# Scan time steps on four column groups with a summing product, and changes of order, banks and queues around it

## The chip, the core and the metric

The kernel runs on one core of one Trainium2 chip. The metric is the device time of one execution in microseconds. Everything is float32. The engines are TensorE (PE, with its weight loads PEld), VectorE (DVE), ScalarE (ACT), GpSimd (POOL) and SyncE (SP), which only issues transfers. Results of TensorE go to eight PSUM banks of 512 columns.

## The reference, cut to what matters

One layer of a decoder step, for a prompt of 256 tokens and eight sampled sequences of 4 tokens (288 columns together):

```
hn   = rmsnorm(h);  proj = hn @ w_in            # z 1024, xbc 1536, dt 16, q/k/v 512 each
xbc  = silu(causal_conv(xbc, conv_state))
dt   = softplus(dt_raw + dt_bias);  a = -exp(a_log)
y    = chunked scan (SSD) of x, dt, a, B, C from state s0; new state is an output
y    = rmsnorm((y + x * d_skip) * silu(z))
att  = block-sparse attention over own keys and paged past keys (1024 per sequence)
h   += concat(y, att) @ w_out
h   += cross attention of rmsnorm(h) over 256 memory tokens, 4 heads, @ w_ca_o
h   += square(relu(rmsnorm(h) @ w_up)) @ w_down
y_prompt, y_sample = rmsnorm(h)
```

Outputs beside y: keys and values of prompt, sample and memory, the convolution histories and the scan states. dt_raw, the "time steps" of the title, is a product of hn (1024 x 288) with 1024 x 16 weights: one value per head and token.

## The kernel before

The activations lie transposed, 128 channels on the partitions and 288 token columns. A dense "tile" is one 128-channel output: eight matmuls of 128 rows x 128 columns of weights against 288 columns of hw (four or eight in the output projections), accumulated in one bank, evicted by VectorE. Weights come in blocks of 1 MB into a ring of four slots (wring), issued by SyncE. In the trace one float32 matmul is two records.

Everything is hand-scheduled: `make_plan` writes one sequence (SEQ) of tiles and items, and each engine walks the same sequence and issues its part of each item. So moving an item moves it on all engines. Small TensorE results go through "turns" (`turn`, `plan_turns`): each turn takes the least recently used bank of a set and waits until that bank's turn before has been evicted by ScalarE or VectorE; the set is TURN_BANKS (2, 3, 6) at the start, FEW_BANKS during the key scores. Banks 0 and 1 alternate for the tiles.

The stages in order, with the names of the items:

- Opening: WARM matmuls of ones into bank 7; ident, x and norm_mix are loaded (L877 to L885); TensorE transposes x (L1146), ScalarE squares it, GpSimd sums the squares (L1001), VectorE scales it by norm_mix into hw (L2080).
- q tiles (L1189), `memt` (transposes of the memory tokens; VectorE scales them, L2080, then ScalarE squares them, L1827, both reading the bank), `ss x` (sum of squares over partitions, L1490, then square root on ScalarE and reciprocal on VectorE, L2152), `qrep` (replication of q, L1577). The q tiles are evicted by two pairs of instructions (L2092, L2094).
- Key scores of the paged keys (L1208, transposed by VectorE, L2229) between tiles of k, memory and x; x tiles are followed by the convolution on VectorE.
- `V` units (L1255): attention probabilities times paged values, four sequences side by side on four column groups of 32.
- `dt`: eight matmuls with wdt (128 x 16 stationary, 288 moving, L1496), then a series on VectorE for softplus, beside the z tiles.
- The scan: `tok` (transposes to token rows), `sums`, `seg`, `yo`, `upd`; `kvtok` writes keys and values as token rows (L1152, L2076) into staging buffers, from which GpSimd stores them (L984). `stage` has two buffers, sq and ohT, so the third group of tokens (sample) uses sq again and waits until the first store out of it has landed (kst_out 0).
- `zsq`: ScalarE squares the gated z and multiplies by the norm's gain (L1827, L1992); `ss ssd`, `inv ssd` (L2152) give the norm's factor. `head self n` is prompt attention; `pvown`/`pvout` combine (L2201) and turn the sampled attention; `state` adds the new scan state (L2380, L2381), `sf` transposes it for the store; `oz`, `oa` tiles are the output projection.
- Cross attention, then the MLP in a form with seven half-width products of sums instead of eight (L1603). Its operands need sums of hw (activation_sum, L2454) and of weights (L2443 and following). VectorE makes the sums of hw while the last output tiles (`cao`) come in.

## Time and profile before

| | us |
|---|---|
| timed runs, median of 3 (lowest to highest) | 657.47 (657.03 to 658.47) |
| the profiled execution: time | 659.61 |
| its span | 658.0 |
| TensorE busy | 631.4 |
| VectorE busy | 404.8 |
| ScalarE busy | 153.5 |
| GpSimd busy | 139.6 |

The span is what the trace covers. Busy times overlap across engines. The mean granted clock of TensorE was 0.991 of full speed. The page's slices show TensorE at nine tenths or more from the second slice to the last but one.

### The profile page before, as it was taken

How to read it: one execution, taken by the hardware profiler on the slowest of the kernel's cores; microseconds unless marked ns; L12 is line 12 of the kernel's file. 1: busy time of each engine (PE TensorE's matmuls, PEld its weight loads, DVE VectorE, ACT ScalarE, POOL GpSimd, SP SyncE). 2: the span in 40 equal slices, each digit the busy share in tenths (PEclk: the TensorE clock that was granted, in tenths of full speed). 3: DMA queues.
4: the chain of work that ended last, by engine and by line, in shares of the span. 5: the costliest groups of instructions: out<-in, count | busy, mean ns of one | idle time of the engine just before them, and what ended most of it. 6: DMA issues, size and time to landing. Idle time of an engine off the chain costs nothing.

```text
span 658.0 us, 13121 instructions
## 1 busy us (share of the span) xinstructions
PE 631.4 (96%) x4879; PEld 505.2 (77%) x4879; DVE 404.8 (62%) x880; ACT 153.5 (23%) x409; POOL 139.6 (21%) x221
## 2 busy tenths in 40 slices
PE   8899999999999999889999999999999999999995
PEld 6656776676676565446757876799999999999995
DVE  2565576997654766685523255878788883644733
ACT  4110020010213974582112433121121110000001
POOL 6142112210310026051001200425344350000000
PEclk8999999999999999899999999999999999999998
DMA  8898878898841259875786653245454454544501
GB/s 297 249 308 266 299 249 271 274 292 244 233 121 65 65 192 293 275 177 152 238 281 256 216 176 120 74 133 179 128 175 147 148 174 161 181 140 133 176 13 73
DMA packets 98636, 125.75 MB, mean 191 GB/s; under 512 B 6428, under 2 KB 74544, under 8 KB 98579
## 3 DMA queue, kind: packets, MB, share of 16 engines
q1 hardware_dynamic: 92930, 106.81, 50.1%
q0 software_dynamic: 5648, 18.14, 8.8%
q8 instruction: 39, 0.64, 0.4%
q14 instruction: 19, 0.15, 0.1%
HBM read 116.63 MB, written 8.31 MB: 190 GB/s over the span
## 4 chain that ended last, share of the span: by engine, by line
PE 73%; DVE 5%; POOL 2%; DMA 2%; issue 1%; ACT 1%; DVEq 0%; POOLq 0%; ACTq 0%
PE ps L1603 33%; PE ps L1189 24%; PE ps L1146 3%; PE ps L1255 3%; DMA out_prompt_k<-sq 2%; PE ps L1208 1%; PE ps L1421 1%; PE ps L1367 1%; POOL acc L1001 1%; PE ps L1303 1%; PE ps L1297 1%; PE ps L1496 1%; PE ps L1411 1%; PE ps L1372 1%; PE ps L1230 1%
## 5 line engine op out<-in xcount | busy, mean ns | idle before, releaser
L1189 PE MATMUL ps<-hw,wring 128*128 128x288 f32 x576 | 148.3, 414 | 0.7 <-DMA wring<-in_w_in 0.6
L1189 PEld LDWEIGHTS ps<-hw,wring 128*128 128x128 f32 x576 | 108.3, 192 | 37.2 <-issue 6.9
L2229 DVE STREAM_TRANSPOSE tmp<-big 128x1024 f32<-128x1024 f32 x32 | 37.9, 1222 | 2.5 <-PE ps L1208 1.9
L1603 PE MATMUL ps<-hw,wring 128*128 128x144 f32 x256 | 34.2, 287 | 1.6 <-DVE hw L2080 1.6
L1001 POOL TENSOR_TENSOR acc<-acc,sq 128x288 f32<-128x288 f32 (+1 forms) x35 | 29.5, 844 | 24.9 <-ACT sq L1827 22.5
L1603 PEld LDWEIGHTS ps<-hw,wring 128*128 128x128 f32 x256 | 32.5, 190 | 2.0 <-DVE hw L2080 2.0
L1603 PE MATMUL ps<-big,wring 128*128 128x144 f32 x256 | 34.0, 286 | 0.0
L2076 DVE COPY tmp<-ps 128x512 f32<-128x512 f32 (+6 forms) x34 | 20.8, 617 | 19.9 <-PE ps L1146 16.1
L1189 PE MATMUL ps<-big,wring 128*128 128x288 f32 x128 | 32.7, 409 | 0.0
L1189 PE MATMUL ps<-attT,wring 128*128 128x288 f32 x128 | 31.9, 407 | 0.7 <-DVE hT L2125 0.7
L1603 PEld LDWEIGHTS ps<-big,wring 128*128 128x128 f32 x256 | 32.4, 190 | 0.0
L1820 ACT ACTIVATE tmp<-ps 128x512 f32<-128x512 f32 (+5 forms) x37 | 20.2, 560 | 49.2 <-PE ps L1146 37.7
L2019 ACT ACTIVATE big<-big 128x288 f32<-128x288 f32 x32 | 13.0, 444 | 74.5 <-DVE big L2641 74.5
L1189 PEld LDWEIGHTS ps<-big,wring 128*128 128x128 f32 x128 | 23.9, 190 | 7.8 <-issue 1.8
L1189 PEld LDWEIGHTS ps<-attT,wring 128*128 128x128 f32 x128 | 24.0, 190 | 7.1 <-DVE hT L2125 0.9
L1189 PE MATMUL ps<-tmp,wring 128*128 128x256 f32 x128 | 29.5, 385 | 0.0
L2622 DVE TENSOR_TENSOR tmp<-ps,xc 128x144 f32<-128x144 f32 x64 | 18.2, 305 | 17.5 <-PE ps L1603 16.4
L832 POOL DMA_DIRECT2D big<-in_cache_k x28 | 15.3, 545 | 63.5 <-issue 63.5
L1124 POOL TENSOR_TENSOR tmp<-big 128x144 f32<-128x144 f32 x16 | 15.5, 969 | 61.9 <-ACT big L2019 61.9
L1189 PEld LDWEIGHTS ps<-tmp,wring 128*128 128x128 f32 x128 | 23.8, 190 | 5.8 <-issue 2.5
L1603 PE MATMUL ps<-tmp 128*128 128x144 f32 x192 | 24.8, 286 | 0.0
L1603 PE MATMUL ps<-tmp,xc 128*128 128x144 f32 x192 | 24.8, 286 | 0.0
(347 smaller groups left out, 1154.3 us busy)
## 6 DMA issues: line engine op xcount, KB each, us to landing
wring<-in_w_in SPq DMA_DIRECT2D x16, 1024.0 KB, 6.8
wring<-in_w_up SPq DMA_DIRECT2D x16, 1024.0 KB, 5.1
wring<-in_w_down SPq DMA_DIRECT2D x16, 1024.0 KB, 4.7
big<-in_cache_v SPq DMA_DIRECT2D x56, 256.0 KB, 3.6
big<-in_cache_k SPq DMA_DIRECT2D x36, 256.0 KB, 3.8
big<-in_cache_k POOLq DMA_DIRECT2D x28, 256.0 KB, 4.5
wring<-in_w_out SPq DMA_DIRECT2D x6, 1024.0 KB, 6.2
wring<-in_w_ca_kv SPq DMA_DIRECT2D x4, 1024.0 KB, 8.7
```

The lines of the kernel that those rows point to most:

```text
L832: e.dma_start(big[:, ds(i * 512 + (n % 2) * 4096, 512)], cache[ds(page, 1)].rearrange("o p n -> p (o n)")).then_inc(signal[n % 2], 16)
L1001: pool.tensor_tensor(a, a, sq[:, m % 2, 0:n], ALU.add).then_inc(acc_done, 1)
L1124: step(pool.tensor_tensor(ff_sums[:, 0, n], a[1], a[0], ALU.subtract))
L1146: last = pe.transpose(ps[0:c, bank(key), col:col + r], in_, ident[0:r, 0:r])
L1189: last = pe.matmul(ps[:, BANK[key], 0:width], w, rhs, start=(k == 0), stop=(k == K_TILES[kind] - 1))
L1255: last = pe.matmul(ps[32 * b:32 * b + 32, PV_BANKS[s], :], p[:, 32 * b:32 * b + 32], src[:, b, t, :], start=((first or again) and t == 0), ...
L1603: last = pe.matmul(ps[:, bank_, col * HALF:(col + 1) * HALF], w(k), x(k), start=(start and k == 0), stop=(stop and k == 3))
L1820: last = act.activation(dst, src, ACT.Copy)
L2019: act.activation(ff[:, c * T:(c + 1) * T], ff[:, c * T:(c + 1) * T], ACT.Square).then_inc(ff_done, 1)
L2076: last = dve.tensor_copy(dst, src)
L2229: dve.transpose(KT_[:, step_ % 2].rearrange("p c (w j) -> p w c j", j=32), src[:, :, :, m, :])\
L2622: return dve.tensor_tensor(w[:, row, half * HALF:half * HALF + HALF], product, part_, ALU.add)
```

## The change

- `dt` is split. A new item `dt_part` stands between the two halves of x tile 5: matmul k goes to column group k mod 4 (32 columns each), so bank rows 0 to 31 hold the part sum of k = 0 and 4, rows 32 to 63 that of 1 and 5, and so on. VectorE copies the bank to vv. At the old place one matmul with a constant 0/1 matrix (dt_sum, 128 x 16) adds the four groups. wdt moves from its own buffer into ohT, padded to 32 columns with zeros that GpSimd sets.
- WARM goes from 12 to 10. ident, x_sample and norm_mix are loaded through ScalarE's queue, and ScalarE computes one square root of a constant at the start, so that its table is loaded there.
- The opening's turns use four banks (2, 3, 6, 7); `memt 0` stands ahead of `ss x`.
- `stage` gets a third buffer, osb; VectorE's wait for kst_out 0 goes, and a wait for kst_out 2 moves from `zsq` on ScalarE to `pvown 0` on VectorE.
- `zsq 0` ahead of `seg 1 3`; `inv ssd` behind `pvout 0`; `oz 0 1` ahead of `sf`.
- The sums 2 and 3 of hw are made once for all four blocks after the last tile, instead of for three blocks ahead of it and one behind.

```diff
-WARM = 12
+WARM = 10
     item("probs", 0)
     pair("x", 4)
     unit("V", 0, 0)
-    pair("x", 5)
+    tile("x", 5, 0)
+    item("dt_part")
+    tile("x", 5, 1)
...
-BANKS_NOW = [TURN_BANKS]
+BANKS_NOW = [[2, 3, 6, 7]]
...
-            IN_SCORES.append(LAST_IN_BANK[6])
+            IN_SCORES.extend(LAST_IN_BANK[b] for b in (6, 7))
...
-        stage = [sq[:, :, :].rearrange("p s t -> p (s t)")[:, 0:512], ohT[:, :]]
+        stage = [sq[:, :, :].rearrange("p s t -> p (s t)")[:, 0:512], ohT[:, :], osb]
...
-            elif kind == "ktok" and key[1] == 2:
-                e.wait_ge(kst_out[0], 16)
...
+                elif s[0] == "dt_part":
+
+                    pe.wait_ge(dtw_in, 16)
+                    pe.wait_ge(wdt_clear, 1)
+                    bank_free(pe, "dt_part")
+                    for k in range(DT):
+                        r = slice(32 * (k % 4), 32 * (k % 4) + 32)
+                        last = pe.matmul(ps[r, bank("dt_part"), 0:T], wdt[:, k, :], hw[:, k, :], start=(k < 4),
+                                         stop=(k >= 4), tile_position=(0, 32 * (k % 4)))
+                    last.then_inc(turn_ps, 1)
                 elif s[0] == "dt":
-                    pe.wait_ge(dtw_in, 16)
+                    turned(pe, "dt_part")
+                    pe.wait_ge(const_in, 16 * 11)
                     tile_bank_free(pe, "dt")
-                    for k in range(DT):
-                        last = pe.matmul(ps[0:SH, BANK["dt"], 0:T], wdt[:, k, :], hw[:, k, :], start=(k == 0), stop=(k == DT - 1))
-                    last.then_inc(dense_ps, 1)
+                    pe.matmul(ps[0:SH, BANK["dt"], 0:T], dt_sum[:, :], vv[:, :], start=True, stop=True).then_inc(dense_ps, 1)
...
+            act.dma_start(ident[:, :], I["ident"]).then_inc(ident_in, 16)
+            for i in range(2):
+                cols = slice(512 * i, 512 * i + 512)
+                act.dma_start(xin[0:NS, 2, cols], I["x_sample"][:, cols]).then_inc(x_in[i], 16)
+                if i == 0:
+                    act.dma_start(vec_rows[0:DT, :], I["norm_mix"].rearrange("(r n) -> r n", n=P)).then_inc(mix_in, 16)
+
+            act.wait_ge(zeros_made, 2)
+            act.activation(small[:, 95:96], eps_t[:, :], ACT.Sqrt)
...
-                    activation_sum(2, 0, 3)
-                    activation_sum(3, 0, 3)
                     step(activation_sum(0, 3, 4))
                 elif c == 7:
                     dve.wait_ge(hw_done, 16 + 8)
                     activation_sum(1, 3, 4).then_inc(hs_made, 1)
                     dve.wait_ge(hs_made, 1)
-                    activation_sum(2, 3, 4)
-                    activation_sum(3, 3, 4).then_inc(hs_made, 1)
+                    activation_sum(2, 0, 4)
+                    activation_sum(3, 0, 4).then_inc(hs_made, 1)
```

TensorE around the time steps, before (L1189 are tiles, eight matmuls each; L1255 is a V unit; L1496 the time steps):

```order
L1189 MATMUL ps<-hw,wring 128x288 x16
L1255 MATMUL ps<-big,qs 32x512 x8
L1189 MATMUL ps<-hw,wring 128x288 x16
L1255 MATMUL ps<-big,qs 32x512 x8
L1496 MATMUL ps<-hw,wdt 16x288 x8
L1189 MATMUL ps<-hw,wring 128x288 x40
```

and now (L1194 are the tiles, L1261 the V units, L1505 the part sums, L1512 the summing product):

```order
L1194 MATMUL ps<-hw,wring 128x288 x16
L1261 MATMUL ps<-big,qs 32x512 x8
L1194 MATMUL ps<-hw,wring 128x288 x8
L1505 MATMUL ps<-hw,ohT 32x288 x8
L1194 MATMUL ps<-hw,wring 128x288 x8
L1261 MATMUL ps<-big,qs 32x512 x8
L1512 MATMUL ps<-vv,tmp 16x288
L1194 MATMUL ps<-hw,wring 128x288 x40
```

The eight part products have moved up between two x tiles, and one product is left behind the V unit.

VectorE after the first prompt heads, before (L2407 to L2409 the bounds of a head, L2152 the reciprocal of the scan's norm, L2201 the combination of sampled attention that TensorE transposes next):

```order
L2407 TENSOR_REDUCE mx<-tmp 128x1
L2408 TENSOR_REDUCE mx<-tmp 128x1
L2409 TENSOR_SCALAR mx<-mx 128x2
L2152 RECIPROCAL rstd<-rstd 128x288
L2201 TENSOR_TENSOR tmp<-ps,qs 128x512
L2076 COPY attT<-ps 64x256
```

and now (L2225 is that combination, L2175 the reciprocal, L2147 the first use of its result):

```order
L2433 TENSOR_SCALAR mx<-mx 128x2
L2225 TENSOR_TENSOR tmp<-ps,qs 128x512
L2099 COPY attT<-ps 64x256
L2438 RECIPROCAL mx<-mx 128x2
L2444 TENSOR_SCALAR tmp<-tmp,mx 128x128
L2444 TENSOR_SCALAR tmp<-tmp,mx 128x256
L2428 SCALAR_TENSOR_TENSOR tmp<-ps,tmp 128x384
L2431 TENSOR_REDUCE mx<-tmp 128x1
L2432 TENSOR_REDUCE mx<-tmp 128x1
L2433 TENSOR_SCALAR mx<-mx 128x2
L2175 RECIPROCAL rstd<-rstd 128x288
L2147 TENSOR_TENSOR vv<-ps,rstd 128x288
```

The reciprocal has moved behind the combination and the next head's bounds, to just ahead of its use.

TensorE at the transposes of the new state, before (L1146 x8 are the transposes, the L1189 row after them is tile oz 0 1):

```order
L1279 MATMUL ps<-kT,qz 128x256
L1146 MATMUL ps<-ident,tmp 128x128 x8
L1189 MATMUL ps<-big,wring 128x288 x8
L1255 MATMUL ps<-big,qs 32x512 x8
L1303 MATMUL ps<-tmp,vtok 64x128 x3
```

and now (L1151 the transposes, L1194 the tile):

```order
L1285 MATMUL ps<-kT,qz 128x256
L1194 MATMUL ps<-big,wring 128x288 x8
L1151 MATMUL ps<-ident,tmp 128x128 x8
L1261 MATMUL ps<-big,qs 32x512 x8
L1309 MATMUL ps<-tmp,vtok 64x128 x3
```

The tile has moved ahead of the transposes.

## Rows read from the trace of the kernel before

**Rows 1.** The page: busy time, share and instructions of each engine.

```profile
PE 631.4 (96%) x4879; PEld 505.2 (77%) x4879; DVE 404.8 (62%) x880; ACT 153.5 (23%) x409; POOL 139.6 (21%) x221
```

**Rows 2.** Waits of TensorE: who waited, for whom, total us, times, longest.

```profile
PE ps L1146 <- ACT sq L1827: 3.3, 2, 1.6
PE ps L1152 <- DVE sq L2076: 2.6, 1, 2.6
PE ps L1146 <- DVE tmp L2381: 1.6, 1, 1.6
PE ps L1603 <- DVE hw L2080: 1.6, 1, 1.6
...
PE ps L1146 <- DVE tmp L2201: 0.9, 1, 0.9
...
PE ps L1490 <- POOL acc L1001: 0.7, 1, 0.7
...
PE ps L1189 <- DMA wring<-in_w_in: 0.6, 1, 0.6
```

**Rows 3.** Timeline of the opening: start, us, engine, line, operation, idle before.

```profile
1.17 4.43 PE L1440 MATMUL ps<-ones 128*128 128x128 f32 x24 [1.17 <-POOL eps_t L1004]
...
3.72 0.43 SPq L854 DMA_DIRECT2D wring<-in_w_in  x1
...
6.96 0.46 DVE L2076 COPY hT<-ps 128x288 f32<-128x288 f32 x1 [0.99 <-PE ps L1146]
...
10.94 5.84 PE L1189 MATMUL ps<-hw,wring 128*128 128x288 f32 x16 [0.55 <-DMA wring<-in_w_in]
```

**Rows 4.** Stretches: busy of each engine, then granted clock, DMA share, GB/s.

```profile
10.00:15.00 5.00, 4.45 (x13) 3.06 (x12) 1.62 (x5) 3.25 (x6) 4.28 (x6) 0.66 1.06 394
255.00:282.00 27.00, 23.52 (x142) 12.22 (x141) 17.20 (x36) 13.49 (x34) 3.14 (x7) 0.94 0.83 262
```

**Rows 5.** Timeline of 25 to 60, at the replication of q.

```profile
31.78 0.86 DVE L2092 TENSOR_TENSOR qz<-ps,rstd 64x256 f32<-64x256 f32 x2 [2.36 <-PE ps L1189]
...
34.51 1.93 PE L1577 MATMUL ps<-qs,ident 128*32 128x256 f32 x32
```

**Rows 6.** Timeline of 160 to 210, at the time steps.

```profile
164.47 1.92 PE L1255 MATMUL ps<-big,qs 128*32 128x512 f32 x16
...
166.22 4.04 PE L1496 MATMUL ps<-hw,wdt 128*16 128x288 f32 x16
...
170.19 20.06 PE L1189 MATMUL ps<-hw,wring 128*128 128x288 f32 x80
...
182.22 7.57 PEld L1189 LDWEIGHTS ps<-hw,wring 128*128 128x128 f32 x32 [0.58 <-DVE big L2103]
```

**Rows 7.** Timeline of 236 to 285, behind the copy of the sample keys.

```profile
265.46 0.68 DVE L2076 COPY sq<-ps 32x512 f32<-32x512 f32 x1 [4.04 <-DMA out_prompt_k<-sq]
...
268.27 2.07 PE L1367 MATMUL ps<-tmp,later 128*128 128x512 f32 x2
...
269.58 1.23 DVE L2288 TENSOR_TENSOR tmp<-tmp,ex 128x1024 f32<-128x1024 f32 x1 [1.17 <-ACT ex L1881]
```

**Rows 8.** Timelines of 274 to 284 and 282 to 352: ScalarE's idle time, the reciprocal.

```profile
280.09 0.60 ACT L1899 ACTIVATE tmp<-ps 128x512 f32<-128x512 f32 x1 [3.39 <-PE ps L1367]
...
292.65 1.94 DVE L2152 RECIPROCAL rstd<-rstd 128x288 f32<-128x288 f32 x1
```

**Rows 9.** Timeline of 404 to 436, VectorE ahead of the first MLP chunk.

```profile
425.90 1.20 DVE L2454 TENSOR_TENSOR kT<-hw,vtok 128x432 f32<-128x432 f32 x1
...
427.84 0.37 DVE L2080 TENSOR_SCALAR hw<-hT,vec 128x288 f32<-128x288 f32 x1
```

**Rows 10.** Value pages: SyncE's issues, TensorE's use, and the page's median landing.

```profile
312.36 23.00 SPq L841 DMA_DIRECT2D big<-in_cache_v  x16
...
339.00 1.93 PE L1255 MATMUL ps<-big,qs 128*32 128x512 f32 x16
...
big<-in_cache_v SPq DMA_DIRECT2D x56, 256.0 KB, 3.6
```

More of the change, by code:

```diff
@@ L148, in make_plan @@
     tile("qk", 0, 1)
+    item("memt", 0)
     item("ss", "x")
-    item("memt", 0)
     tile("qk", 1, 0)
@@ L237, in make_plan @@
     unit("V", 0, 2)
+    item("zsq", 0)
     item("seg", 1, 3)
-    item("zsq", 0)
     item("yo", 1, 2)
@@ L249, in make_plan @@
     item("head", "self", 0)
-    item("inv", "ssd")
     item("pvown", 0)
@@ L253, in make_plan @@
     item("pvout", 0)
+    item("inv", "ssd")
     tile("oz", 0, 0)
@@ L257, in make_plan @@
     item("head", "self", 2)
+    tile("oz", 0, 1)
     item("sf")
-    tile("oz", 0, 1)
     unit("V", 1, 0)
@@ L424, in plan_turns @@
             turn("conv")
+        elif s[0] == "dt_part":
+            turn("dt_part", "dve")
         elif s[0] == "kvtok":
@@ L582, in build @@
         cvin = part(1536)[0:NB * 3, :]
+        dt_sum = part(SH)
         CS = tmp[:, 0:1024].rearrange("p (s t) -> p s t", s=2)
@@ L605, in build @@
         ebuf = ohT[:, :]
+        wdt = ohT[:, 0:DT * 32].rearrange("p (k n) -> p k n", k=DT)
         at[0] = xpad_at
@@ L740, in bank_free @@
                 turned(e, BEFORE_IN_BANK[key])
-            elif bank(key) in UP_BANKS:
+            elif bank(key) in UP_BANKS[:2]:
                 e.wait_ge(up_done, 16)
@@ L914, in load_constants @@
                     sp.dma_start(hcol[:, i:i + 1], I[name].rearrange("(h o) -> h o", o=1)).then_inc(const_in, 16)
-                sp.dma_start(wdt[:, :, :], w_in[:, IN_DT:IN_DT + SH].rearrange("(k p) n -> p k n", p=P))\
+                sp.dma_start(wdt[:, :, 0:SH], w_in[:, IN_DT:IN_DT + SH].rearrange("(k p) n -> p k n", p=P))\
                     .then_inc(dtw_in, 16)
@@ L1007, in _ @@
             pool.memset(qw, 0.0).then_inc(qw_clear, 1)
+            pool.memset(wdt[:, :, SH:32], 0.0).then_inc(wdt_clear, 1)
             add_squares("x", T)
@@ L1070, in _ @@
                         turned(pool, (outs[0][0], g))
-                        store(kd, stage[g % 2][0:n, :] if s[0] == "kvtok" else mstage[0:n, g],
+                        store(kd, stage[g][0:n, :] if s[0] == "kvtok" else mstage[0:n, g],
                               kst_out[g if s[0] == "kvtok" else 3 + g])
@@ L1196, in key_steps @@
                     if k == 0 and g == 0:
-                        turned(pe, IN_SCORES[0])
+                        for key in IN_SCORES:
+                            turned(pe, key)
                         tile_done(pe, ("qk", 0, 1))
@@ L1698, in turn_targets @@
                 return xKT[:, u[1], c, 2 * w:2 * w + 2, :], ps[:, b, :].rearrange("p (b t) -> p b t", b=2)
+            if kind == "dt_part":
+                return vv[:, :], ps[:, b, 0:T]
             if kind == "qrep":
@@ L2200, in take_result @@
                     if s == 0:
+                        dve.wait_ge(kst_out[2], 16)
                         dve.tensor_tensor(osb, ps[:, 7, :], qsf[:, 0:512], ALU.add).then_inc(pv_out, 1)
@@ L2556, in _ @@
                     self_bounds(s[1])
+                elif s[0] == "dt_part":
+                    leave("dt_part")
                 elif s[0] == "dt":
```

17 lines of the change are left out of this document (7 added, 10 removed).

## The prediction

> **What bounds the kernel now.** I read the page first: TensorE is busy for 631.4 of 658.0 us [rows 1]. So time can only come from shorter matmul work, from TensorE's few waits, or from its clock. The waits of TensorE come next [rows 2]: seven lines, 11.3 us. The reader is to see that each is named by one producer, and that four producers (the squares of ScalarE, the copy to sq, the new state, the down-scaled hw) are other engines' instructions that stand behind something TensorE doesn't need yet. Then the timeline around each of them [rows 3, 5 to 10], and the granted clock [rows 4]. Between those places TensorE has no idle time, so what is taken away in one place arrives at the end whole, unless a transfer has a date of its own.
>
> The sum is made against the profiled execution: span 658.0, time 659.61. The median of the timed runs is 657.47, 2.14 under that time; I subtract the same gain from it.
>
> **Part by part.**
>
> *Opening.* Four small transfers leave SyncE for ScalarE's queue, which has nothing to do there; w_in then stands third on SyncE instead of seventh. It was issued at 3.72 [rows 3]; four issues fewer, of about 0.43 each [rows 3], make it 1.7 earlier. But the same bytes must pass before it, so it lands 0 to 1.7 earlier. Two warm-up matmuls fewer are 4 of 24 records, at 4.43 / 24 0.7 at most; the last ones run faster than the mean, I take 0.45. The first tile, which waited 0.6 for w_in [rows 2], starts no earlier than TensorE's own work lets it: 0.6 + 0.45, about 1.1. I take 0.5; ends 0 and 1.1. The square-root table is loaded early; TensorE isn't waiting there, so I cost it at nothing.
>
> *Four banks instead of three, memory transposes ahead of the sum of squares.* With three banks a transposition of memory waits for the one two before it, whose last reader is a square on ScalarE, behind a scaling on VectorE, behind the evictions of q. That is 3.3 in two equal waits, one before the last q tile and one after it [rows 2]. With four banks TensorE runs through both. Then the replication of q (34.51) is next [rows 5]: it needs the eviction of the last q tile (from 31.78, 0.86 for one pair and about 0.4 for the other, so to 33.0; now 31.4, since its tile starts 1.6 earlier) and the bank of the fifth memory transposition, a scaling and a square later: about 32.2. Gain 34.5 - 32.2 = 2.3; I take 2.2. Ends: 1.0 (VectorE later by two scalings more) and 3.3.
>
> *Time steps on four column groups.* Before: sixteen records, 4.04 [rows 6]. New: eight matmuls of 32 columns, four side by side. The row for this pattern is L1255: sixteen records of 512 columns, started at 164.47, followed at 166.22, 1.75; scaled to 288 columns 1.0. The summing product is two records of 288 columns at 20.06 / 80 = 0.25 each [rows 6], 0.5, plus about 0.3 where it starts and ends a mode. 4.0 - 1.8 = 2.2; I take 2.1. Ends: -2.5 (no cost of the changes), and +0.6 (no concurrency: 4.0, plus 0.5, plus 0.1). The extra copy of 128x288 costs VectorE 0.46 [rows 3]; it lies beside a tile of 4.0 whose eviction and convolution leave VectorE about 1 us, so it is hidden. If that cover were gone it would cost 0.46. The series on VectorE that follows starts behind the eviction of the first z tile, which moves by as much as TensorE. The eviction after the series is the one that TensorE just meets at 182.22 [rows 6]; it keeps its distance, and is what is late next.
> Rows 6 already hold one entry to column groups and one exit. The Trainium skill, TensorEngine Tiling (Array Packing), "Key Properties", says that changing the tiling mode drains TensorE, and the change adds such a switch pair in the middle of a stretch of full tiles. By the drain seen in rows 6 it is small; by a drain as long as a tile the gain of this step would be gone. The same page, "PSUM Bottleneck", warns that the copy out becomes the limit; here that is the 0.46 above, beside other work.
>
> *The third staging buffer.* VectorE's copy of the sample keys stood 4.04 until a store out of sq had landed [rows 7], and TensorE behind it 2.6 [rows 2]. The new target (osb) waits for nothing. The copy then comes at about 262.0, the last transposes follow the others without a gap, and the whole chain on ScalarE and VectorE behind it moves by 2.6. The wait for the copy's own store moves to VectorE's first combination of attention values, just behind the reciprocal at 292.65 [rows 8], some 30 us later. Ends 2.2 and 2.8.
>
> *The clock there.* After that idle stretch the clock is at its lower level (1.2 of 2.4 GHz) for part of 255 to 282: mean 0.94 [rows 4], so 27 times 0.06, 1.6 us worth of full-speed cycles lost; L1367 takes 2.07 [rows 7]. Without the idle time I expect no fall. But ScalarE and VectorE set the pace there (the weighted x at 269.58 doesn't depend on that matmul [rows 7]), so I count 0.6; ends 0 and 1.6.
>
> *Squares of z earlier, reciprocal later.* The first pair of squares fits ScalarE's 3.39 of idle time before 280.09 [rows 8]; the sum on GpSimd ends 1.0 earlier and TensorE's 0.7 [rows 2] goes, but the first head's probabilities are ready no earlier, so little of it counts. The reciprocal (1.94) stood ahead of the combination that TensorE awaited 0.9 [rows 2]; it goes behind it, and is done before the first output tile (4.0) ends. Together 0.8; ends 0.4 and 1.6.
>
> *State transposes behind a tile.* TensorE waited 1.6 for the new state [rows 2]. A tile of 4.0 now stands ahead of it, and covers it: 1.5; ends 0.8 and 1.6.
>
> *Activation sums.* Two subtractions of three blocks, the second 1.20 long, stood ahead of the last hidden-state update, whose scaling at 427.84 TensorE awaited 1.6 [rows 2, 9]. They are now done for all four blocks after it. What is late next is their own product; between the release of the first sums and it lie two products of eight half-width records (1.0 each by rows 6) and the sum of squares (0.5), 2.5, against 1.20 x 4 / 3 = 1.6 and half of that for the two longer subtractions, 2.4. It just fits. 1.5; ends 0.6 and 1.6.
>
> Sum: 0.5 + 2.2 + 2.1 + 2.6 + 0.6 + 0.8 + 1.5 + 1.5 = 11.8. Span 646.2; time of a run 657.47 - 11.8 = 645.7.
>
> **The rivals.**
>
> *A, the waits come back as others.* Three of the places (27 to 36, 266 to 282, 289 to 306) have VectorE or ScalarE close behind TensorE. If a reordered instruction is next in line there, half of 2.2 + 0.6 + 0.8 + 1.5 + 1.5 = 6.6 is lost: 649.0. For: the chains are long. Against: in each I find the next producer at least 0.2 earlier.
>
> *B, the column groups don't run side by side* with different moving operands, so the change doesn't do what it says: +0.6 instead of -2.1, 648.4. Against: L1255 has different moving operands too, and its 1.75 is a quarter of sixteen full records.
>
> *C, the values arrive late.* SyncE issues sixteen pages from 312.36 in 23.00, the last at 335.4; a landing takes 3.6, so 339.0, and TensorE uses them at 339.00 [rows 10]. There is no slack at all. Both ends hang on the same instruction, so an equal shift keeps them together; but a slower stretch of SyncE, with everything around it moved, costs up to 1 to 2: 647.
>
> *D, the clock stays up in the opening too.* It fell for part of 10 to 15 (mean 0.66 [rows 4]), after the wait for w_in; the first tile took 5.84 against 4.0 for a tile [rows 3, 6]. If it doesn't fall, 1.8 more: 643.9.
>
> *E, slower than before: the clock falls for long.* With fewer warm-up matmuls and a thin opening (transposes of 128 columns), TensorE may be granted the lower level through the opening. Each tile then costs 4.0 more. To cancel 11.8 it has to be held there for 23.6 us of busy work, so from 11 to about 36; as a stretch through the opening that gives 657 to 660. The Trainium skill, TensorE: Matmul & The Clock Gate, "What's actually happening", says that the slow state is the default and activity releases it, which speaks against taking warm-up work away. Against: in rows 4 the clock came back by itself during the first tile.
>
> **How the numbers follow.** The forecast (645.7, its own range 643.9 to 647.8) gets 0.68; A 0.12; B 0.05; C 0.05; D 0.07; E 0.03. The range 643.5 to 650.0 takes in A to D and leaves out E and combinations of A with others. A change of 0.2% (1.3 us) is what a measurement of this kernel can tell: every case but E is faster by more, so faster 0.95; for the same I leave 0.02, a half-way E; slower 0.03.
>
> **What would show it.** Right: the waits of TensorE fall from 11.3 to about 2 or 3; sixteen records of the new product end within 1.1 us of their start; no wait of TensorE for ScalarE's squares; VectorE's copy of the sample keys waits for no store; mean clock 1.00 in the stretch that was 255 to 282; TensorE's busy time falls by 3 to 5. Wrong, step by step: a wait of TensorE on a memory scaling before the replication of q over 0.5; a wait before tile (z, 1, 1) over 0.5; the first chunk of the up projection waiting for the second pair of sums; a time above 650 with those waits gone, which could only be the clock or a transfer.

## The result, and the profile after

| | before | changed |
|---|---|---|
| timed runs, median (lowest to highest) | 658.47 (657.03 to 659.51), 5 runs | 652.05 (649.15 to 652.41), 5 runs |
| the profiled execution: time, span | 659.61, 658.0 | 650.07, 648.4 |
| mean granted clock of the profiled execution | 0.991 | 0.997 |

The ratio is 0.9895, with a 95% interval of 0.9869 to 0.9921: faster by 1.05%. I had forecast 645.7 (643.5 to 650.0), so the direction holds and the size does not. Two numbers stand out. The gain in the profiled executions is 9.6 us, in the medians 6.4: the profile of before is of a run above its median (659.61), that of the changed kernel of one below it (650.07). And three of the five timed runs lie at 652.1 to 652.4 with a mean clock of 0.986, while the profile is of one at 0.997. That 0.997 is too high; why is said at the opening below.

The page, TensorE's busy time (answers to [rows 1]):

```profile
PE 629.1 (97%) x4877; PEld 504.6 (78%) x4877; DVE 405.7 (63%) x879; ACT 152.3 (23%) x409; POOL 139.0 (21%) x222
```

The waits of TensorE in the changed kernel (for whom, total us, times, longest; answers to [rows 2]):

```profile
PE ps L1592 <- ACT sq L1842: 1.5, 1, 1.5
...
PE ps L1151 <- DMA vec_rows<-in_norm_mix: 1.0, 1, 1.0
...
PE ps L1194 <- DVE big L2126: 0.4, 1, 0.4
```

Of the seven lines with 11.3 us that I had counted, one is left, the squares of ScalarE, with 1.5 instead of 3.3. Two are new: 1.0 for norm_mix in the opening, and 0.4 on an eviction. Together that is 2.9. Waits on other producers, which I had not counted, are nearly as before.

The two timelines can be laid side by side, because TensorE does nearly the same work in the same order. The table follows the start of the same TensorE instruction in both; where the distance changes, time was won or lost. It is the most useful reading of this case.

| at | before | changed | changed minus before | won in this part | forecast |
|---|---|---|---|---|---|
| second q tile | 16.70 | 19.43 | +2.73 | -2.7 | 0.5 |
| replication of q (L1577, now L1592) | 34.51 | 35.00 | +0.49 | 2.2 | 2.2 |
| first z tile, behind the time steps | 170.19 | 168.57 | -1.62 | 2.1 | 2.1 |
| transposes of z-stage results (L1146) | 190.09 | 188.75 | -1.34 | -0.3 | 0 |
| first product behind the staged keys (L1367) | 268.27 | 264.13 | -4.14 | 2.8 | 2.6 |
| same chain, later (L1400) | 283.42 | 278.80 | -4.62 | 0.5 | 0.6 (clock) |
| behind the first combination (L1146) | 295.38 | 289.32 | -6.06 | 1.4 | 0.8 |
| values, first unit of group 1 (L1255) | 309.36 | 301.44 | -7.92 | 1.9 | 1.5 |
| sum of squares in the MLP (L1645) | 430.33 | 420.83 | -9.50 | 1.6 | 1.5 |

Behind the opening 12.2 us are won, where I had forecast 11.3. Between 309 and 425 the distance does not change by 0.1. Nearly the whole miss stands in the first row.

The opening of the changed kernel (answers to [rows 3]):

```profile
1.17 4.64 PE L1446 MATMUL ps<-ones 128*128 128x128 f32 x20 [1.17 <-POOL eps_t L1008]
...
1.84 0.57 ACTq L1931 DMA_DIRECT2D vec_rows<-in_norm_mix  x1
1.94 0.46 SPq L862 DMA_DIRECT2D wring<-in_w_in  x1
...
6.82 0.24 PE L1151 MATMUL ps<-ident,vec_rows 8*128 8x8 f32 x1 [1.02 <-DMA vec_rows<-in_norm_mix]
...
7.00 6.95 PE L1151 MATMUL ps<-ident,xc 128*128 128x128 f32 x24
...
13.88 5.63 PE L1194 MATMUL ps<-hw,wring 128*128 128x288 f32 x16
```

norm_mix is issued earlier than before (1.84 instead of 2.36), yet TensorE can use it only at 6.82, where the kernel before had transposed it at 5.56. w_in is now issued at 1.94, but it is hardly w_in that travels beside norm_mix. The packets up to 5.5 us, in the changed kernel:

```profile
DMA packets 666, 1.06 MB, mean 193 GB/s; under 512 B 50, under 2 KB 180, under 8 KB 666
...
q1 hardware_dynamic: 470, 0.93, 49.5%
q10 hardware_dynamic: 196, 0.13, 8.5%
```

q10 is ScalarE's queue, q1 SyncE's. The packets of w_in have 1 KB, those of x_prompt 2 KB, those of ident and norm_mix 512 B. Between 512 B and 2 KB there are 180 - 50 = 130, ident's 128 and the first two of norm_mix's eight; w_in has none yet, its first starts at 5.55. norm_mix's eight packets move between 5.0 and 6.03, in the kernel before between 4.0 and 4.93. What now runs ahead of them and beside them is the second half of x_prompt, issued at 1.44 instead of 2.77 because no small transfer stands before it on SyncE. (No run separates the two: none takes the small transfers off SyncE and holds x_prompt or w_in back.)

TensorE stands 1.02 us behind a shorter warm-up. Then its transposes take 0.29 each, against 2.24 / 12 = 0.19 before. The page gives the clock as 1.00 there, but the trace holds no clock entry before 16.91 in this execution, and a stretch without an entry is shown as full speed. The durations tell the level: TensorE was at the lower one (1.2 of 2.4 GHz) through the transposes and most of the first tile. So the mean of 0.997 leaves out the opening. 16.9 us at half the clock are 0.5 x 16.9 / 648.4 = 0.013 of the span, which makes it about 0.984 (an estimate). In this execution the level did not rise during the warm-up at all.

The other places, in the changed kernel's timeline of TensorE (and one row of VectorE), answers to [rows 5 to 8]:

```profile
35.00 1.93 PE L1592 MATMUL ps<-qs,ident 128*32 128x256 f32 x32 [1.50 <-ACT sq L1842]
...
161.07 1.18 PE L1505 MATMUL ps<-hw,ohT 128*32 128x288 f32 x16
162.17 4.15 PE L1194 MATMUL ps<-hw,wring 128*128 128x288 f32 x16
...
167.99 0.65 PE L1512 MATMUL ps<-vv,tmp 128*16 128x288 f32 x2
168.57 11.91 PE L1194 MATMUL ps<-hw,wring 128*128 128x288 f32 x48
180.88 3.42 PE L1194 MATMUL ps<-hw,wring 128*128 128x288 f32 x13 [0.40 <-DVE big L2126]
```

```profile
260.63 0.68 DVE L2099 COPY tmp<-ps 32x512 f32<-32x512 f32 x1 [0.55 <-PE ps L1157]
```

```profile
283.88 0.75 PE L1496 MATMUL ps<-acc,ones 128*128 128x288 f32 x2
...
289.32 0.60 PE L1151 MATMUL ps<-ident,tmp 128*128 128x128 f32 x4
...
300.48 1.04 PE L1151 MATMUL ps<-ident,tmp 128*128 128x128 f32 x8
...
417.58 2.43 PE L1618 MATMUL ps<-hw,wring 128*128 128x144 f32 x16
```

The stretch that answers to the second of [rows 4] (TensorE busy, granted clock, DMA share, GB/s):

```profile
262.00:280.00 18.00, 16.50 (x114) 1.00 0.78 266
```

The sixteen records of the new product are followed after 162.17 - 161.07 = 1.10, the summing product after 168.57 - 167.99 = 0.58: 1.7 instead of 4.0. The copy of the sample keys waits for TensorE, no longer for a store, and behind it the clock stays at 1.00. The sum on GpSimd, the combination, the new state and the last scaled hw (rows at 283.88, 289.32, 300.48, 417.58) are met without a wait.

### The profile page after: what moved, and what is told of

It reads as the page before. It is cut to its first block, busy times and chain, and to the rows that moved or that the text cites. A ratio compares the mean times of both kernels' runs of the same rounds, so it can differ in the third digit from the quotient of the medians.

```text
span 648.4 us, 13116 instructions
## 1 busy us (share of the span) xinstructions
PE 629.1 (97%) x4877; PEld 504.6 (78%) x4877; DVE 405.7 (63%) x879; ACT 152.3 (23%) x409; POOL 139.0 (21%) x222
## 4 chain that ended last, share of the span: by engine, by line
PE 77%; DVE 3%; ACT 1%; issue 1%; DVEq 0%; ACTq 0%
PE ps L1618 34%; PE ps L1194 25%; PE ps L1151 4%; PE ps L1261 3%; PE ps L1427 1%; PE ps L1214 1%; PE ps L1373 1%; PE ps L1309 1%; PE ps L1157 1%; PE ps L1303 1%; PE ps L1285 1%; PE ps L1417 1%; PE ps L1406 1%; PE ps L1236 1%; PE ps L1292 1%
## 5 line engine op out<-in xcount | busy, mean ns | idle before, releaser
L1194 PE MATMUL ps<-hw,wring 128*128 128x288 f32 x576 | 148.4, 413 | 0.4 <-DVE big L2126 0.4
L1194 PEld LDWEIGHTS ps<-hw,wring 128*128 128x128 f32 x576 | 108.1, 192 | 37.3 <-issue 6.9
L1194 PE MATMUL ps<-big,wring 128*128 128x288 f32 x128 | 32.7, 409 | 0.0
L1194 PE MATMUL ps<-attT,wring 128*128 128x288 f32 x128 | 31.9, 407 | 0.7 <-DVE hT L2148 0.7
L1194 PEld LDWEIGHTS ps<-big,wring 128*128 128x128 f32 x128 | 23.9, 190 | 7.9 <-issue 1.8
L1194 PEld LDWEIGHTS ps<-attT,wring 128*128 128x128 f32 x128 | 24.0, 190 | 7.1 <-DVE hT L2148 0.9
L1194 PE MATMUL ps<-tmp,wring 128*128 128x256 f32 x128 | 29.5, 385 | 0.0
L1194 PEld LDWEIGHTS ps<-tmp,wring 128*128 128x128 f32 x128 | 23.8, 190 | 5.9 <-issue 2.5
```

Of the source, the lines that this page charges most:

```text
L1194: last = pe.matmul(ps[:, BANK[key], 0:width], w, rhs, start=(k == 0), stop=(k == K_TILES[kind] - 1))
```

## The experiments

The runs of the kernel before on the same chips had medians of 657.5 to 658.7. Its own spread is 3 to 5 us, and that of the variants 1.3 to 9, so that each kernel's list of runs says more than its median. In the diffs, - is the kernel that the experiment starts from.

### The opening taken apart

e1 puts the whole opening of before back into the changed kernel, e2 only the warm-up rounds, e3 only the queue (and leaves the early square root out); e4 puts the new opening into the kernel before.

```
e1, e2   -WARM = 10                              +WARM = 12
e1, e3   -act.dma_start(ident ...), 2 x x_sample, norm_mix; act.activation(.. Sqrt)
         +sp.dma_start(ident ...), 2 x x_sample, norm_mix   (ahead of w_in)
e4       the kernel before, with WARM = 10, those four on act, and the square root
```

> The changed kernel with the opening of the kernel before: 12 warm-up rounds, the four small transfers on SyncE, no early square root; all else as changed. Theory O (the opening is the step that failed): the first row after the opening, which stood 2.7 us later than before in the profile, comes back to its old place; the PE wait on the vector of norm_mix (1.0) goes, the 24 transposes take about 4.5 instead of 6.95, and the time is 12.3 under the kernel before, about 646. Rival P (what the timed runs lack, 6.4 gained against 9.6 in the profile, is lost at some later place): still 649 to 652. Rival C (the clock rises or falls by chance in the opening, whatever the opening is): the time spreads by 2 us or more between runs as that of the changed kernel does.

> The changed kernel with 12 warm-up rounds instead of 10 (24 records instead of 20); the small transfers stay on ScalarE's queue. Theory W (two warm-up rounds fewer let the clock stay at its lower level): TensorE is at the upper level during the transposes, which take about 4.5, and the time is 646 to 648. Rival Q (it is the transfers: norm_mix lands late behind w_in and x): the wait on norm_mix stays about 0.5 to 1.0 and so does most of the loss, 649 to 652.

> The changed kernel with the four small transfers back on SyncE ahead of w_in, and no early square root; the warm-up stays at 10 rounds. Theory W: the clock stays low through the transposes, they take about 7, 649 to 652. Rival Q: the vector lands by 5.3, TensorE goes straight from the warm-up into the transposes and the clock is up from the first of them; 646 to 648.

> The kernel before with the changed opening alone (10 warm-up rounds, the four small transfers on ScalarE's queue, the early square root). If the opening costs 2.7 by itself: slower than before by 1 to 3 (some of it may be hidden by the two waits of 1.63 on ScalarE's squares that follow, but those chains start later too), 659 to 661. By my prediction: 0.5 faster, 658.

| | median | runs | 
|---|---|---|
| changed | 652.05 | 649.15, 650.07, 652.05, 652.32, 652.41 |
| e1: opening of before | 648.22 | 647.02, 647.74, 648.22, 648.32, 648.36 |
| e2: 12 rounds | 646.05 | 646.01, 646.04, 646.05, 646.56, 647.93 |
| e3: queue of before, 10 rounds | 647.99 | 647.00, 647.98, 647.99, 649.52, 650.47 |
| e4: before, with the new opening | 661.77 | 660.70 to 663.38 (7 runs) |

Theory O holds in its place: in e1 the wait for norm_mix is gone and the second q tile is at 16.38 (before 16.70). With either half of the opening put back, 4 to 6 us come back, and the new opening alone makes the kernel before slower (ratio 1.0046, 1.0026 to 1.0067), at 661.77 a little above the 659 to 661 of my expectation, where my prediction had it 0.5 faster. Rival P, as the only cause, is refuted. But W and Q both fall as single causes: ten rounds do no harm with the old queue (e3 has the median of e1, with more spread), and the new queue does none with twelve (e2 is 2.2 below e1). It is the two together. e2's opening:

```profile
1.17 4.87 PE L1446 MATMUL ps<-ones 128*128 128x128 f32 x24 [1.17 <-POOL eps_t L1008]
...
6.79 0.20 PE L1151 MATMUL ps<-ident,vec_rows 8*128 8x8 f32 x1 [0.75 <-DMA vec_rows<-in_norm_mix]
...
6.91 4.41 PE L1151 MATMUL ps<-ident,xc 128*128 128x128 f32 x24
...
11.25 4.15 PE L1194 MATMUL ps<-hw,wring 128*128 128x288 f32 x16
```

norm_mix lands at the same time, but the transposes take 4.41 instead of 6.95 and the first tile 4.15 instead of 5.63: 4.0 of lower level gone. With w_in on time and the clock up, this execution has a span of 644.4. e1's opening is that of before: at the upper level through the transposes, a wait of 0.28 for w_in at 10.62, and then the lower level for part of the first tile.

```profile
10.62 5.84 PE L1198 MATMUL ps<-hw,wring 128*128 128x288 f32 x16 [0.28 <-DMA wring<-in_w_in]
```

e1 came out at 648.22 and not at the 646 that I had expected, and its trace shows why. I had costed the early square root at nothing, and e1 and e3 are without it. In e1:

```profile
22.09 1.28 ACT L1833 ACT_TABLE_LOAD   x1
...
30.83 0.74 PE L1155 MATMUL ps<-ident,mkv 128*128 128x128 f32 x4 [0.82 <-ACT sq L1846]
```

and in e2:

```profile
2.82 1.28 ACT L1934 ACT_TABLE_LOAD   x1 [2.82 <-issue]
```

In the kernel before this load stood at 13.82, in idle time of ScalarE. Now `memt 0` stands ahead of `ss x`, so without the early square root the load comes behind the first squares of memory and ahead of the square root that the scaling of q waits for. From the second q tile to the replication of q e1 takes 32.91 - 16.38 = 16.53 and e3 16.52, where e2 and the changed kernel take 15.57: 0.96 of the gain of the four banks hangs on the early square root. With the 1.06 that e1 lacks at the second q tile these are 2.0 of the 2.3 between the two spans (646.7 and 644.4).

### The slower runs of the changed kernel

e12 is the changed kernel once more.

> The changed kernel as it is, once more, for the clock of its other runs: three of its five runs took 652.3 at a mean clock of 0.986 while its profile is of one at 650.07 and 0.997. Theory W: the profile or the runs show the lower level somewhere in the first 20 us, with longer transposes or tiles there, and all else as in the first profile. Rival P: a second stretch at the lower level at a later place (as the one of 3.4 us at 267 of the kernel before).

Six runs, median 651.38 (648.63, 649.04, 650.63, 652.13, 652.18, 652.68); the profile is of the run at 652.13, with the clock of 0.986. TensorE's stretches (busy, granted clock, DMA share, GB/s), then its rows:

```profile
8.00:18.00 10.00, 10.00 (x30) 0.51 0.93 331
...
219.00:228.00 9.00, 9.00 (x55) 0.81 0.35 118
```

```profile
6.79 0.20 PE L1151 MATMUL ps<-ident,vec_rows 8*128 8x8 f32 x1 [1.38 <-DMA vec_rows<-in_norm_mix]
6.92 6.11 PE L1151 MATMUL ps<-ident,xc 128*128 128x128 f32 x24
12.95 6.88 PE L1194 MATMUL ps<-hw,wring 128*128 128x288 f32 x16
...
222.72 5.84 PE L1194 MATMUL ps<-hw,wring 128*128 128x288 f32 x16
```

Both theories were half right. The lower level in the opening is the same loss (second q tile at 19.76, first profile 19.43), here with entries in the trace: it rose during the warm-up, at 4.86, and fell at 8.27, behind the 1.38 of idle time. And there is a second fall, at 223, behind a series of 32-column products, in a full tile (5.84 instead of 4.15): 1.7. Together 2.0, the 2.1 between the spans 650.5 and 648.4. Six of the changed kernel's eleven runs lie at 652.1 to 652.7 with this mean clock (0.986), so they probably carry both; only this one has a trace.

### The other parts, undone one at a time

All start from e2.

```
e5  -BANKS_NOW = [[2, 3, 6, 7]]                 +BANKS_NOW = [TURN_BANKS]     (and memt 0 behind ss x)
e6  -item("dt_part"); dt_sum product            +8 matmuls of wdt in "dt", wdt in a buffer of its own
e7  -stage = [sq.., ohT[:, :], osb]             +stage = [sq.., ohT[:, :]]    (and the waits of before)
e8  zsq 0 behind seg 1 3; inv ssd ahead of pvown 0; sf ahead of tile oz 0 1
e9  -activation_sum(2, 0, 4), (3, 0, 4)         +(2, 0, 3), (3, 0, 3) early, (2, 3, 4), (3, 3, 4)
```

> The changed kernel with 12 warm-up rounds (646.05 in its own runs), and the turns of the opening on three banks again, memory transposes behind the sum of squares. If the term holds by itself (2.2; the trace of the changed kernel shows 2.24 between the second q tile and the replication of q): 648.2, and TensorE waits twice 1.6 for ScalarE's squares again. Rival S (the wait of 1.5 that the changed kernel still has ahead of the replication of q belongs to the same chain, and takes the gain back when the clock is up): 646.0 to 647.

> The changed kernel with 12 warm-up rounds, and the time steps in one product of 16 records again, from a buffer of its own. If the term holds: the trace of the changed kernel gains 2.1 there and gives 0.28 back to a wait on VectorE's eviction behind it, so 1.8 slower, 647.9. Rival S (the gain is paid back by that wait when more of the kernel is on time): 646.5.

> The changed kernel with 12 warm-up rounds, and two staging buffers for the keys again: VectorE's copy of the sample keys waits for a store. Stage term alone: 2.8 slower, and the clock falls in that place as before, another 0.5: 649.3. Rival S (the clock does not fall there although TensorE idles 2.6): 648.8, mean clock 1.00 in the 15 us behind the wait.

> The changed kernel with 12 warm-up rounds, and three places of the order as before: the first squares of z behind the last segment, the reciprocal ahead of the first output combination, the state transposes ahead of the tile (oz, 0, 1). From the traces these give 1.4 and 1.9, together 3.3: 649.3, with the waits on GpSimd's sum (0.7), on the combination (0.9) and on the new state (1.6) back. Rival S (they share one slack behind them): half of it, 647.7.

> The changed kernel with 12 warm-up rounds, and the activation sums 2 and 3 in two parts as before (three blocks ahead of the last one). If the term holds: 1.6 slower, 647.6, with the wait of 1.6 on the last scaled hw ahead of the up projection back. Rival S: the wait is there but less, since VectorE is ahead: 646.5.

| | median | fastest, minus e2's fastest (646.01) | highest | forecast of the part |
|---|---|---|---|---|
| e5 three banks | 650.51 | 648.12: 2.1 | 651.87 | 2.2 |
| e6 one dt product | 648.19 | 648.11: 2.1 | 649.78 | 2.1 |
| e7 two stages | 649.25 | 648.90: 2.9 | 650.57 | 3.2 (with the clock) |
| e8 three orders | 650.34 | 649.42: 3.4 | 654.62 | 2.3 |
| e9 sums | 648.01 | 647.32: 1.3 | 654.06 | 1.5 |

The medians of e5 and e8 are raised by openings at the lower level, so I compare the fastest runs. The five parts sum to 11.8, and none gives its gain back to another, but for the 0.3 behind the time steps that e6's expectation has: rival A and rival B are refuted, and rival S for each edit too (in e7 by the clock in the trace, since the times for it and for the term lie too close). The places show it: in e5 the two waits of 1.6 on ScalarE's squares are back, and from the second q tile to the replication it takes 32.85 - 15.04 = 17.81, in e2 30.89 - 15.32 = 15.57, 2.24 less. In e7 TensorE waits 2.03 for the copy, and behind it the clock is down:

```profile
262.00:276.00 14.00, 13.70 (x81) 0.90 0.62 207
```

against 1.00 in e2's same stretch. Undoing the wait removes the fall, and bringing it back brings the fall back; it costs about as little as I had counted: TensorE is 2.24 behind e2 at the copy and 2.87 a few us later, 0.6 more. In e8's and e9's traces the other parts stand as in the table: 0.6 and 0.9 at the sum and the combination and 1.9 at the new state, and 1.6 at the sums of hw.

In e9, where the profile fell on the slowest run, the level rose at 5.15 and fell at 8.56 although the kernel has twelve rounds:

```profile
7.10 0.19 PE L1151 MATMUL ps<-ident,vec_rows 8*128 8x8 f32 x1 [1.10 <-DMA vec_rows<-in_norm_mix]
7.23 6.12 PE L1151 MATMUL ps<-ident,xc 128*128 128x128 f32 x24
13.28 6.86 PE L1194 MATMUL ps<-hw,wring 128*128 128x288 f32 x16
```

So twelve rounds lessen the loss and don't exclude it. e8's profile, of its slowest run, has the same fall at 9.98 with only 0.25 of idle time, behind a level that had risen late, at 6.56. e4's has it at 9.75, behind a rise at 6.34, within its idle time of 0.82. All three of e8, e9 and e12 have the second fall too, at 221.6 to 223.6.

### Number of rounds, or idle time behind them

```
e10  e2, norm_mix first on ScalarE's queue      e15  the same with WARM = 14
e11  the changed kernel, WARM = 14              e14, e18b  WARM = 16            e16  e2 once more
e13  the changed kernel (WARM = 10), -pe.wait_ge(zeros_made, 1)  +pe.wait_ge(zeros_made, 3)
```

> The changed kernel with 12 warm-up rounds, and norm_mix as the first transfer on ScalarE's queue, ahead of the identity. Theory L (TensorE's wait of 0.75 is for norm_mix, late behind x_sample's bytes and w_in's): the wait goes, but the transposes need the identity and x next, which then come 0.5 later; 645.4 to 646. Rival M (all small transfers are late alike, behind the large ones): no change, 646.05, a wait for another of them in its place.

> The changed kernel with 14 warm-up rounds (28 records). TensorE's idle time ahead of the norm_mix transpose (0.75 with 12 rounds) takes about 0.4 to 0.75 of the four records more, so at the upper level they cost 0 to 0.2. Theory W (warm-up work decides the clock): the clock is up in every run, no run over 646.6, median 646.1. Rival C (chance decides): the spread of 2 us stays.

> The changed kernel with its 10 warm-up rounds and its queues, but the warm-up waits for GpSimd's third fill too, so that it starts at about 2.9 instead of 1.17 and ends at about 7, where norm_mix has landed: as many rounds, no idle time behind them. Theory G (the idle time between warm-up and transposes is what costs: TensorE stands 1.0 to 1.4 there, and the clock is down at 8 to 10 or never up): the transposes take 4.4 to 5.5, no run at a mean clock under 0.99, time 646.5 to 648.5. Theory W (ten rounds are too few): the clock stays low through the transposes, 650 to 653.

> The changed kernel with 16 warm-up rounds (32 records). Theory G: no idle time behind the warm-up, the clock is never under 0.995 in the mean, but the transposes start later by the records that stand past the landing of norm_mix (4 records more than with 14 rounds, 0.6 to 0.9): 647 to 648. Theory W (more rounds, better clock): no better than 14 rounds can be told, 646.5 to 647. Rival C (chance): a run at 0.99 or lower among the five.

> The changed kernel with norm_mix first on ScalarE's queue and 14 warm-up rounds. With 12 rounds this order ran into low clocks in five of six runs (649.4 to 655.1), with 0.5 of idle time between the norm_mix transpose and the first x transposes. Theory G: with 14 rounds the warm-up ends where x lands, the idle time is under 0.1, and the times are those of the 14 rounds without it, 645.9 to 647.5. Rival X (the order of the transfers itself, by the traffic it makes, lowers the clock): still 649 or more in most runs.

> The changed kernel with 12 warm-up rounds once more (first time: 646.05, 646.01 to 647.93), because four kernels that differ from it only far behind the opening had single runs 2.4 to 6.7 above their fastest. Theory G: of five runs one to three are above 648, those with the clock at 0.995 or lower; the median lies between 646 and 649. Rival (twelve rounds are enough, the others were chance): all five under 648.

> The changed kernel with 16 warm-up rounds once more, beside the kernel with the early replication on the same chip. Theory G (no idle time behind the warm-up): 646.1 to 646.5 in most runs, none at 649 or more. Rival C (chance): a run at a mean clock under 0.993.

| new queue, with | median | runs | TensorE idle ahead of or among the first transposes, in the profile |
|---|---|---|---|
| 10 rounds (changed, e12) | 652.05 | 11 runs, 648.63 to 652.68 | 1.02; 1.38 |
| 12 rounds (e2, e16) | 647.2 | 10 runs, 646.01 to 649.88 | 0.75; 0.78 |
| 14 rounds (e11) | 646.82 | 645.91 to 648.18 | none |
| 16 rounds (e14, e18b) | 646.6 | 10 runs, 646.12 to 648.20 | 0.20; none |
| 10 rounds, started at 2.94 (e13) | 647.10 | 646.12, 646.15, 647.10, 648.51, 650.12 | none |
| norm_mix first, 12 rounds (e10) | 651.39 | 645.78, 649.45, 650.95, 651.83, 652.39, 655.06 | 0.50 |
| norm_mix first, 14 rounds (e15) | 650.01 | 646.72, 647.81, 648.22, 651.80, 652.11, 653.56 | 0.49 |

e13 tells it most plainly: ten rounds as in the changed kernel, moved so that they end where norm_mix lands, give 647.1 instead of 652. (It moves the start of the warm-up too, and no run takes the idle time away and leaves start and number as they are.)

```profile
2.94 3.88 PE L1446 MATMUL ps<-ones 128*128 128x128 f32 x20 [2.94 <-POOL qz L1009]
6.77 0.21 PE L1151 MATMUL ps<-ident,vec_rows 8*128 8x8 f32 x1
6.91 4.41 PE L1151 MATMUL ps<-ident,xc 128*128 128x128 f32 x24
```

Theory G (the idle time) explains more than W (the number), but not all. One run of e13 at 650.12 is outside what G expected (it was not the one profiled), and e8 had its fall with 0.25 of idle time. In the changed kernel's first profile the level never rose before the idle time, so there the idle time had nothing to lose. Run by run, against what was expected:

- e11: W wanted no run over 646.6; three of its five runs are (646.82, 647.56, 648.18), and the spread of 2 us stays, as rival C had it. Its profile is of the slowest. It is 0.7 behind e2 at the second q tile, because the level rose only at 7.40 and stretched the warm-up to 6.34, and lost 1.2 more in one gap between two key scores at 58, which has nothing to do with the opening.
- e14: G wanted 647 to 648 for the records past the landing; they cost nothing that can be told (646.26). Its one run at 648.20 had a mean clock of 0.994, a little under G's 0.995.
- e16: as G expected, two of five runs above 648.
- e10: theory L wanted 645.4 to 646 and rival M 646.05. The fastest run, which is the profiled one, is L's (645.78, norm_mix in use at 5.91 right behind the warm-up); five of six are 3.7 to 9.3 above it, which neither expected.
- e15: the idle time of 0.5 stayed, and three of six runs still took 651.8 or more, as rival X had it for most. With norm_mix first, the first part of x_sample is issued at 1.93 and lands at 6.58 (e10) and 6.71 (e15); in e2, issued at 1.38, it had landed at 5.31. So the new order lets TensorE wait for x_sample instead of norm_mix.
- e18b: the times were up to 647.54, a little above what I expected, with the clock at 0.995 or more; its level rose only at 5.65, which stretched its 32 records to 5.96 us and moved the transposes to 7.21, 0.5 later than in e14.

What e10's five runs at 649.45 to 655.06 and e15's three at 651.80 to 653.56 lost is not seen. e10's profile lost nothing, and e15's (648.22) nothing in the opening either: its second q tile is at 15.16, ahead of e2's 15.32, and it lost 1.7 in a fall of the clock at 240, in a tile behind narrow products, as e3's profile did at 243. So neither profile shows a loss behind the 0.5 us, and that the order of transfers itself (rival X) has a part isn't excluded.

### The wait that was left

```
e17b  WARM = 16;  -item("memt", 3), item("qrep")   +item("qrep"), item("memt", 3)
```

> The changed kernel with 16 warm-up rounds (646.26), and the replication of q ahead of the last memory transposes: there TensorE still waits 1.5 for a bank that ScalarE's square of memory releases. In the trace with 16 rounds the last eviction of q ends at 29.65 and the replication starts at 30.73. Theory: it starts at about 29.8, 0.9 earlier, and the last transposes follow without a wait: 645.3. Rival: the sum of squares of memory then comes late, or a tile behind it waits for the cache's transfers, and the 0.9 is a wait there: 646.2.

646.13 (645.62 to 647.56), beside e18b at 646.96 (646.27 to 647.54) on the same chip. The ranges overlap; the trace is sharper.

```profile
30.41 1.93 PE L1592 MATMUL ps<-qs,ident 128*32 128x256 f32 x32 [0.92 <-DVE qs L2117]
```

The wait is 0.9 and for the eviction of q, no longer for a square. From the second q tile (15.86) to the tile behind the replication (32.77) it takes 16.91, in e18b 33.06 - 15.62 = 17.44: 0.5 won of 0.9 expected. Against the kernel before on its chip it is at 0.9819 (0.9789 to 0.9849), 5.9 under the changed kernel's median; by the times alone it can't be told from e14 (646.26) or from e2's first five runs (646.05).

## Why the prediction was right or wrong

- *Opening: wrong, and the step that failed.* I wrote that w_in would land up to 1.7 earlier once four small transfers had left SyncE, and took 0.5 won with the ends 0 and 1.1. It measured 2.7 lost in the profile. Three things were wrong in it. I followed w_in and the first tile, and not the first thing that TensorE needs, norm_mix: it came 1.3 later, behind the second half of x_prompt, which moved up as w_in did. I counted the warm-up records as time that TensorE gets back (0.45); behind a shorter warm-up it only waits longer. And I gave the clock the good end only: the lower level through the opening, 4.0 of the 4.1 between the changed kernel's second q tile and e2's, stood at nothing in the sum. That w_in is then on time was right: the changed kernel's first tile waits for it no more.
- *The early square root*, costed at nothing, is worth 1.0 by the traces of e1 and e3, but only together with the memory transposes ahead of the sum of squares; the 2.2 of the four banks contains it.
- *Rival E* had the mechanism, "fewer warm-up matmuls, the lower level through the opening", and I gave it 0.03. Its size was wrong: I wanted it slower than before, 23.6 us at the lower level; it holds to 16.9 or 18.5 and costs about 4. As a loss inside my forecast it would have given 646.2 + 0.5 + 2.7 = 649.4 for the span; the measured 648.4 is 1.0 less, nearly the 0.9 by which the parts behind the opening were better than forecast. The Trainium skill, TensorE: Matmul & The Clock Gate, "What's actually happening", which I had set beside it, calls the lower level the default that activity releases; the first profile agrees, with a level that had not risen before 16.91. What the runs add is that a warm-up which ends too early can lose it again (e12, at 8.27).
- *Rival D* (the level stays up, 1.8 more, 643.9) is what e2's profile looks like: my span of 646.2 less 1.8 is 644.4, e2's span is 644.4. That these agree so well is luck: e2 won 1.4 in the opening where D has 2.3, and 12.2 behind it where D has 11.3. And e2 has twelve rounds, so it is not the kernel that I predicted.
- *Four banks:* 2.2 forecast, 2.24 in the trace, 2.1 when undone, and by the way that I wrote: the replication was to start at 32.2, when the square has freed the bank; it starts at 35.00, less the opening's 2.73 at 32.27. The wait of 1.5 for that square was in this sum, and only my list of signs ("no wait of TensorE for ScalarE's squares") had forgotten it.
- *Time steps:* 2.1 forecast, 2.1 measured, and 0.3 given back to VectorE's eviction at 180.88, which I had named as late next and costed at nothing. The switch of tiling mode costs next to nothing: 1.10 from the sixteen narrow records to the next tile's start, 1.0 by my scaling.
- *Third staging buffer and the clock:* 2.6 and 0.6 forecast, 2.8 and 0.5 in the profile, 2.9 for both when undone.
- *Squares of z and reciprocal; state transposes:* 0.8 and 1.5 forecast, 1.4 and 1.9 in the profile, 3.4 when undone. Too low: I took half of the waits of 0.7 and 0.9 as lost again, and a little of the 1.6 for the new state, and they were not.
- *Sums:* 1.5 forecast, 1.6 in the profile, 1.3 when undone. The first up chunk does not wait for the second pair.
- *Rival C* (values late) has begun to show as TensorE gains on SyncE: no wait in the changed kernel's profile, 0.6 in e15, 0.8 in e16, 0.95 in e13. In e13:

```profile
328.03 1.92 PE L1261 MATMUL ps<-big,qs 128*32 128x512 f32 x16 [0.95 <-DMA big<-in_cache_v]
```

Of the signs that I had named, the waits (11.3 to 2.9), the sixteen records (1.10), VectorE's copy and the clock behind it came as written. TensorE's busy time fell by 2.3 and not by 3 to 5, since the opening's transposes and first tile took 4.0 longer at the lower level; in e2's page it is 625.3, 6.1 less than before, so the 3 to 5 fit neither. And "a time above 650 with those waits gone, which could only be the clock or a transfer" is the sign of being wrong that came true, with both of its causes.

What stays open: why the second fall at 223 comes in some executions and not in others, and what most runs of e10 and half of e15's lost. None of the traces shows what the one run of e13 at 650.12 lost, and the 0.25 of idle time hardly explains e8's fall in the opening. When the level rises seems to matter: idle times of 0.49 to 0.78 were followed by no fall behind rises at 4.44 to 5.46 (the profiles of e2, e5, e7, e10, e15, e16), and 0.25 came with a fall behind a rise at 6.56. No experiment sets that moment, so this is not shown.

## What to carry to other kernels

Taking small transfers off a queue lets the large ones behind them start earlier, and the small ones can land later for it: look first for the earliest thing that the bounding engine needs, and see when that lands, not when it is issued. A warm-up should last until the first real work is ready: here a shorter one saved nothing, and the level was lost behind the idle time, or had not risen. An instruction that is costed at nothing because no engine waits for it (the early square root) can carry another part of the change; undoing it together with its neighbours hides that, and the trace shows it. Laying the same instruction of both traces side by side, and reading where their distance changes, sizes every part of a compound change to about 0.1 us, when medians with a spread of 2 us can't.

## What the runs showed of the hardware

- The instant at which the clock first rises differs between executions that do the same until then: warm-up of TensorE from 1.17 on in all of these, first entry at the upper level at 4.15 (e14), 4.86 (e12), 5.22 (e2), 5.65 (e18b), 6.94 (e6), 7.40 (e11), and 16.91 in the changed kernel's first profile.
- A stretch at the start for which the trace has no clock entry reads as 1.00 although TensorE is at the lower level: transposes of 0.29 in the changed kernel's profile against 0.18 to 0.19 at the upper one.
- A transfer of 4 KB moved at 5.0 to 6.03 and was awaited until 6.82 when issued at 1.84 on ScalarE's queue, with both halves of x_prompt (0.5 MB each) issued by 1.44 on SyncE's; it moved at 4.0 to 4.93 and was in use at 5.56 when issued at 2.36 on SyncE's queue between the two halves.
- The level fell in the opening with idle times of TensorE far shorter than the stretch of low clock that followed: 1.38 (e12, low from 8.27 to 18.51), 1.10 (e9), and 0.25 (e8, low from 9.98 to 16.80); and at 223 with none (e12: TensorE busy for 9.00 of 9.00 us from 219).
- Four column groups with different moving operands do run side by side: 1.10 for sixteen records of 288 columns, against 4.04 before.
